# Seven-product perceptron: VectorE forms a unit's activation sums behind its square, then the weights' low half, then the same unit's low part

## What is computed

```python
hm = rms_norm(x, norm_mlp[l]) @ mlp_w1[l]      # 1024 -> 4096
x = x + jnp.square(jax.nn.relu(hm)) @ mlp_w2[l]  # 4096 -> 1024
```

## Time and profile before

| | |
|---|---|
| median of 3 runs | 1798.84 us (1796.53 to 1799.79) |
| the profiled execution | 1800.41 us, span 1798.6 us |
| TensorE busy | 1742.8 us, 97% of the span |
| TensorE's granted clock, mean | 0.989 |
| VectorE, ScalarE, GpSimd busy | 1116.3, 538.4, 1025.0 us |
| chain that ended last | TensorE 81%, VectorE 14% |
| its largest VectorE line | the weights' low half, L3405, 2% |
| DMA | 97 GB/s over the span |

### The profile page before, as it was taken

How to read it: one execution, slowest core, us unless ns; L and a number is a source line. 1 busy time by engine, 2 the same in 40 slices (tenths; PEclk the granted TensorE clock), 3 DMA queues, 4 the chain that set the end, 5 groups by cost and what they waited for, 6 DMA issues and landing times.

```text
span 1798.6 us, 25531 instructions
## 1 busy us (share of the span) xinstructions
PE 1742.8 (97%) x9082; PEld 1452.8 (81%) x9082; DVE 1116.3 (62%) x1722; ACT 538.4 (30%) x1018; POOL 1025.0 (57%) x780
## 2 busy tenths in 40 slices
PE   6999999999999999999999999989999998989897
PEld 4888888888988888888888778877878786868686
DVE  4754736565455445554553697897375588787878
ACT  4121221211232223222221227545343432222323
POOL 3657555699655444545457668975064744546361
PEclk9999999999999999999999999999999998999999
DMA  9523222385432223232223332201131243232301
GB/s 349 179 81 94 78 80 76 94 321 164 129 93 82 76 73 94 84 89 76 64 78 104 95 85 59 71 19 30 48 89 53 83 164 118 69 117 71 118 24 47
DMA packets 258925, 176.13 MB, mean 98 GB/s; under 512 B 5856, under 2 KB 241184, under 8 KB 257568
## 3 DMA queue, kind: packets, MB, share of 16 engines
q1 hardware_dynamic: 251776, 151.01, 28.1%
q10 hardware_dynamic: 7072, 24.07, 3.7%
HBM read 172.31 MB, written 2.62 MB: 97 GB/s over the span
## 4 chain that ended last, share of the span: by engine, by line
PE 81%; DVE 14%; ACT 2%; issue 2%; SPq 1%; DMA 1%; ACTq 0%; DVEq 0%
PE acc L425 12%; PE acc L427 12%; PE acc L426 12%; DVE wl L3405 2%; PE sc L1814 2%; PE acc L473 2%; PE acc L474 2%; PE acc L475 2%; DVE mlp_low L3399 2%; PE acc L2481 2%; PE acc L2482 2%; PE acc L2480 2%; SPq L749 1%; PE acc L455 1%; PE acc L456 1%
## 5 line engine op out<-in xcount | busy, mean ns | idle before, releaser
L873 POOL TENSOR_SCALAR wh<-raw 128x1024 fp32r<-128x1024 f32 (+1 forms) x168 | 193.6, 1153 | 491.8 <-PE acc L427 139.5
L876 POOL TENSOR_TENSOR wl<-raw,wh 128x512 fp32r<-128x512 f32 x328 | 455.8, 1410 | 14.0
L425 PE MATMUL acc<-hh,wh 128*128 128x512 f32 x672 | 275.5, 410 | 0.1
L427 PE MATMUL acc<-hh,wl 128*128 128x512 f32 x672 | 263.8, 393 | 0.0
L426 PE MATMUL acc<-hl,wh 128*128 128x512 f32 x672 | 263.1, 392 | 0.0
L425 PEld LDWEIGHTS acc<-hh,wh 128*128 128x128 f32 x672 | 127.3, 189 | 29.1 <-POOL wl L876 1.7
L427 PEld LDWEIGHTS acc<-hh,wl 128*128 128x128 f32 x672 | 126.9, 189 | 27.9
L426 PEld LDWEIGHTS acc<-hl,wh 128*128 128x128 f32 x672 | 127.3, 189 | 27.3 <-issue 2.4
L725 POOL TENSOR_TENSOR mlp_blocks<-mlp_blocks 128x512 f32<-128x512 f32 x32 | 52.8, 1671 | 110.2 <-DVE wl L3405 109.2
L2480 PE MATMUL acc<-hh,wh 128*128 128x512 f32 x256 | 99.9, 390 | 0.4 <-ACT mlp_kept L1571 0.4
L2482 PE MATMUL acc<-hh,wl 128*128 128x512 f32 x256 | 99.7, 389 | 0.0
(11 more groups left out here) (620 smaller groups left out, 4294.0 us busy)
## 6 DMA issues: line engine op xcount, KB each, us to landing
raw<-in_att_w_in SPq DMA_DIRECT2D x64, 512.0 KB, 3.9
raw<-in_ret_w_in SPq DMA_DIRECT2D x48, 512.0 KB, 3.9
raw<-in_mlp_w SPq DMA_DIRECT2D x32, 512.0 KB, 4.0
mlp_blocks<-in_mlp_w SPq DMA_DIRECT2D x16, 1024.0 KB, 5.0
ada_w<-in_ada_w ACTq DMA_DIRECT2D x8, 1536.0 KB, 7.2
raw<-in_w_in SPq DMA_DIRECT2D x23, 512.0 KB, 3.6
ada_w<-in_ada_w SPq DMA_DIRECT2D x16, 512.0 KB, 9.3
raw<-in_ret_w_out SPq DMA_DIRECT2D x16, 512.0 KB, 3.6
```

The lines of the kernel that those rows point to most:

```text
L425: e.matmul(bank[:, :], wh[:, s, k, :], rhs_high(k), start=(start and k == 0), stop=False)
L427: last = e.matmul(bank[:, :], wl[:, s, k, :], rhs_high(k), start=False, stop=(stop and k == k1 - 1))
L873: e.tensor_scalar(wh[:, s, 0:k1, :], raw[:, s, 0:k1, :], 1.0, 1.0, ALU.mult, ALU.mult).then_inc(high_done, 1)
L876: low = e.tensor_tensor(wl[:, s, k0:k0 + KT // 2, :], raw[:, s, k0:k0 + KT // 2, :], wh[:, s, k0:k0 + KT // 2, :].bitcast(F32), ALU.subtract)
```

## The change

VectorE's list for a unit was: square; from unit 4 on the low half of weights; the low part of the unit before; the unit's sums; in units 5 and 7 a block sum. It becomes: square; sums; from unit 4 on the low half of weights; the low part of the same unit; in units 5 and 7 the block sum. The low part of the last unit, which stood behind the loop, is in it.

```diff
--- before.py
+++ after.py
@@ -3424,11 +3424,10 @@
             for q in range(QUARTERS):
                 for j in range(IN_UNITS):
                     squared(q, j)
+                    combos(q, j)
                     if j >= 4:
                         weights_low(q, (j - 4) // 2, (j - 4) % 2)
-                    if j:
-                        combos_low(q, j - 1)
-                    combos(q, j)
+                    combos_low(q, j)
                     if j >= 5 and j % 2:
                         block_sum(e, V, q, (j - 5) // 2, 1)
                     if q == 0 and j == 2:
@@ -3437,7 +3436,6 @@
                         roots(e, 0, NT, None)
                         step(e, e.tensor_tensor(rs[:, 0, 0:NT], rs[:, 0, 0:NT], rs[:, 0, 0:NT], ALU.mult), V, "nfroot")
                         step(e, e.tensor_scalar(fneg[:, :], rs[:, 0, 0:NT], -1.0, None, ALU.mult), V)
-                combos_low(q, IN_UNITS - 1)
                 for i in range(PRODUCTS):
                     if i + 2 < PRODUCTS:
                         weights_low(q, i + 2, 0)
```

## The result

The changed kernel takes 1780.34 us (median of 4 runs, 1779.26 to 1783.29); the kernel before took 1799.32 in the same series. The ratio is 0.9899, its 95% interval 0.9882 to 0.9917: faster by 1.0%.

A forecast was written before the change was run, and what follows sets the result against it. VectorE's order was taken to stall TensorE: 4.4 us a quarter, 17.6 in four, less 0.8 for the clock, gain 16.8; 1800.41 becomes 1783.6, the median 1.57 lower: 1782.0 us, range 1773 to 1790.

The forecast's parts named there:

- The ring: Square, weights' low half, previous low part, sums, ScalarE's rounding, next relu wait in a circle; VectorE idles 5.08 us a window.
- The window: VectorE's stretch from unit 4's square to the end of product 0's addition: 33.8 us before, 29.5 us forecast.
- the new wait for the rounding: VectorE's low part waits for ScalarE's rounding: 0.19 us in each of four units, 0.76 us.
- the contention: VectorE instructions wait beside GpSimd's block sums: two lose about 1.1 us each per sum, again 4.2 us a window.
- Units 0 to 3: VectorE's square, sum, ScalarE's rounding and low part take 5.1 us, below the 5.44 us pace; nothing passes to unit 4.
- The clock: TensorE may run at 1.2 GHz after the stall before product 2: 0.2 us a quarter, 0.8 us, bounds 0 and 3.4.
- the two terms: VectorE's gain before product 2, 17.6 us over four quarters, and TensorE's slower clock behind that stall, costing 0.8 us.
- a lock term: Uncertainty of what VectorE loses beside GpSimd's block sums: 0.55 us a quarter either way.
- The lighter lock: Rival: GpSimd's block sums fall into VectorE's waits, up to 2.2 us more a quarter, 8.8 in all: 1773 us; chance 0.15.
- The clock's case: Rival: TensorE stays at the low level through all of product 2, about 1795.5 us; chance 0.08.
- The case of no effect: Rival: product 2 waits for something other than VectorE's order, so nothing changes; chance 0.02.
- The starved GpSimd: Rival: VectorE holds back product 1's block sum over 7 us, then halts 4.85 us twice a quarter: 1803.6 us; chance 0.05.

The follow-up runs named there:

- the third experiment: Against the kernel before: new VectorE order for units 0 to 3 only, old order for units 4 to 7; 1797.02 us, ratio 0.9986.
- the repeated run: The changed kernel measured once more, with no further edit; 1781.44 us, ratio 0.9903 to the kernel before.
- the run with four parts: Against the changed kernel: GpSimd's half of each block sum in four instructions of 256 columns instead of two of 512; 1779.37 us, ratio 0.9891 to the kernel before.

## Why the prediction was right

**What bounds it.** The ring and VectorE's place in it were right, and two runs show which half of the change opens it: the sums forward give everything, the low part moved alone nothing.

**The time.** 1782.0 us were forecast, within 1773 to 1790; 1780.34 came, and 1781.44 in the second series.

**The window.** 29.5 us were forecast, 29.3 came. Term by term: the waits for the relus and for the weights' rounding vanished (5.08 us); the new wait for the rounding was taken as 0.19 us and is 0.21; the contention was taken as 4.2 us in four instructions, a low part and the next square in each block sum, and is 1.03 + 1.09 + 1.03 + 1.08 = 4.2 in just these. One term was left out, that unit 3's low part leaves the window (0.6 us, some 2.5 us in the time by the third experiment), and one was not itemized, the short gaps between instructions that now stand back to back, as the 0.04 us between a square and its sums; they come to some 0.3 us, an estimate from what is left of 29.3. That the two partly cancel was luck.

**Units 0 to 3.** I gave the low part 1.77 us in a chain of 5.1. It takes 1.00 us behind a wait of 0.70:

```profile
1542.30 1.00 DVE L3399 TENSOR_TENSOR mlp_low<-mlp_kept,mlp_high 128x512 fp32r<-128x512 f32 x1 [0.70 <-ACT mlp_high L1578]
```

GpSimd's two instructions run from 1539.72 to 1542.75, so most of the second falls into VectorE's wait for ScalarE. The chain is 1539.09 to 1543.30, 4.2 us. Wrong by 0.9 us, without effect, as it stays below the pace of 5.44 either way.

**TensorE.** Inside product 1 there is no stall in the quarters 1 to 3 and 0.59 us in the first. Before product 2 it waits 2.6 us (some 3 forecast). Product 3 follows product 2 after 6.58 us in the third and fourth quarter (6.59 forecast), and later in the first two, as told under the clock. The squares of unit 4 lie 1544.53 - 1458.12 = 86.4 us apart in two quarters (86 forecast, 90.4 before).

**The clock.** 0.8 us were taken for it. The granted clock by stretch, just behind product 2's start in the first to fourth quarter, and in the second quarter of the repeated run:

```profile
1487.56:1490.50 2.94, 2.94 (x9) 2.32 (x10) 2.81 (x2) 1.06 (x1) 2.77 (x3) 0.66 0.00 0
1573.90:1577.10 3.20, 3.20 (x8) 2.52 (x9) 3.07 (x2) 1.06 (x1) 3.03 (x3) 0.50 0.00 0
1660.20:1663.40 3.20, 3.20 (x14) 2.67 (x15) 3.07 (x2) 1.06 (x1) 2.74 (x3) 1.00 0.01 3
1746.09:1749.30 3.21, 3.21 (x14) 2.69 (x15) 3.08 (x2) 1.06 (x1) 3.04 (x3) 1.00 0.00 0
```

```profile
1576.81:1580.00 3.19, 3.19 (x14) 2.65 (x15) 3.06 (x2) 1.06 (x1) 3.02 (x3) 1.00 0.00 0
```

The level was low (0.50, 1.2 GHz) after one stall of 2.61 us and full after two more of the same length and after one of 2.62. In the first quarter it fell too, shortly behind the restart: 0.66 is a mean over both levels, after a stall of 2.68 us. The repeated run has the low level in its third and fourth quarter, after 2.62 and 2.61 us. So it fell in two of four quarters in each of the two profiles, and why in these stays open. Where it was low, product 3 came 0.56 to 0.67 us later (1494.74 - 1487.56 = 7.18 in the first quarter instead of 6.51 before, 1581.04 - 1573.90 = 7.14 in the second instead of 6.58). The size of the term, 0.3 to 0.85 a quarter where it falls, holds.

**The sum.** Forecast gain 16.8 us. The perceptron became 17.5 us shorter in the profiles, and the medians moved by 19.0 in the first series and 17.4 in the second. By its interval the first series allows 14.9 to 21.2 us, so the 19.0 contradict nothing, and the stretch in front of the perceptron scatters by 5.4 us between the profiles. In the profiles the two terms can be read apart. From product 1's start to product 2's the four quarters became 4.55, 4.49, 4.49 and 4.52 us shorter, 18.05 against the 17.6 forecast. From product 2's start to product 5's they took 0.56 us more than before, against the 0.8 for the clock: part of the lateness of product 3 is made up again behind it. Together that is 17.5. One step of the sum was too wide: a lock term of 2.2 us either way and a clock term between 0 and 3.4 give 1779.0 to 1786.8, not 1778 to 1788.

**The rivals.** The lighter lock did not come: both block sums cost their full 2.1 us. It came in the run with only the sums forward, where VectorE waits for relus while GpSimd works. The clock's case did not come: the low level lasted some 3.2 us behind a stall of 2.6, not all of product 2. The case of no effect is out by the interval. The starved GpSimd did not come: its block sums take 3.79 and 3.80 us from their release, where 7 would have been needed. The Trainium skill (SBUF — State Buffer, section on the two separate sides) says that the one that started first holds the shared ports for its whole instruction. The runs agree that the one waits for the other, and add what that rule leaves open: with both engines always ready the instructions alternate, and VectorE loses 1.03 to 1.09 us each time at 512 columns and 0.38 to 0.53 at 256. That the whole instruction counts they do not show: held up by nothing, GpSimd takes 1.25 us for 512 columns (two in 2.50, at 1572.21 in the changed kernel) and 0.94 for 256 (four in 3.76, at 1571.23 in the run with four parts), more than VectorE loses, and its 0.84 us at 8 columns cost VectorE nothing.

## What to carry to other kernels

When two engines hand each other work in a ring through in-order queues, first give the other what it waits for, last take what it returns, and put independent work as long as the round trip between: exchanging two steps decided over the whole 1%. Once the ring is open, the work of the engine that is left is the bound: moving 0.7 us a unit to an engine with room, and halving the instructions that it contends with, brought another 0.8%. A delay by one unit also hides the round trip, but leaves one more step behind the last unit.

## What was not expected of the hardware

Halving GpSimd's instructions did not only spread the contention, it lowered it: from 2.1 to 1.7 or 1.8 us in a block sum, though GpSimd itself then took 4.71 us instead of 3.79. With 8 columns it was gone, though GpSimd's instructions still showed 0.84 us each. So what VectorE loses does not follow from the length that the profile shows for GpSimd's instruction. And waiting shelters from it: an instruction of VectorE that had to wait for ScalarE anyway was 1.00 us long beside a busy GpSimd, where it had been 1.77 (0.68 where it lost nothing, unit 3's at 1553.59 in the kernel before).
